# The first down product as seven products in turn, with its weight sums made in the projections

## What is computed

```python
h2 = _rmsnorm(x, norm2_w) * (1.0 + scale2) + shift2
ffn = jnp.dot(jax.nn.silu(jnp.dot(h2, w_ffn_gate)) * jnp.dot(h2, w_ffn_up), w_ffn_down)
x = x + gate2 * ffn
...
return _rmsnorm(x, final_norm_w)
```

## Time and profile before

| | |
|---|---|
| median of 3 runs | 1528.05 us (1527.63 to 1528.16) |
| profiled execution | 1528.31 us, span 1526.4 us |
| PE busy | 1509.9 us, 99% |
| DVE busy | 951.3 us, 62% |
| ACT busy | 634.2 us, 42% |
| transfers | 197.58 MB, mean 129 GB/s |

### The profile page before, as it was taken

The page is one execution under the profiler, slowest core; times in us unless marked ns, Lnnn a source line. Parts: engine busy times, 40 slices in busy tenths (PEclk is TensorE's granted clock), DMA queues, the critical chain, the costliest instruction groups (busy, mean ns, idle before and its releaser), DMA issues.

```text
span 1526.4 us, 21071 instructions
## 1 busy us (share of the span) xinstructions
PE 1509.9 (99%) x8593; PEld 1234.8 (81%) x8593; DVE 951.3 (62%) x1680; ACT 634.2 (42%) x1065; POOL 44.3 (3%) x82
## 2 busy tenths in 40 slices
PE   7999999999999999999999999999999999999999
PEld 5777887778888898888888887877788988888887
DVE  6679886765367666435333376787567456556885
ACT  4453334653322442222232253766525334434652
POOL 0000000000000000000000011200011000000000
PEclk9999999999999999999999999999999999999999
DMA  9322122136345258666522215100113232232463
GB/s 386 143 83 97 56 70 83 56 129 244 129 160 180 76 183 277 236 221 218 196 97 97 83 33 221 56 29 30 56 56 124 97 99 85 92 111 97 134 223 133
DMA packets 64042, 197.58 MB, mean 129 GB/s; under 512 B 5956, under 2 KB 6084, under 8 KB 62792
## 3 DMA queue, kind: packets, MB, share of 16 engines
q1 hardware_dynamic: 63944, 196.22, 37.3%
HBM read 182.57 MB, written 13.63 MB: 129 GB/s over the span
## 4 chain that ended last, share of the span: by engine, by line
PE 93%; DVE 4%; ACT 1%; DMA 1%; issue 1%; SPq 0%; DVEq 0%
PE bank L669 89%; PE bank L681 4%; DVE AR L1936 1%; DVE wl L1909 1%; DMA raw<-in_wst 1%; DVE G L1943 0%; DVE AR L2246 0%; DVE ST L1936 0%; DVE X L1936 0%; ACT AR L1779 0%; ACT wh L1370 0%; DVE Hl L1936 0%; ACT L1779 0%; DVE X L1943 0%; DVE PRMT L1936 0%
## 5 line engine op out<-in xcount | busy, mean ns | idle before, releaser
L1370 ACT ACTIVATE wh<-raw 128x1024 fp32r<-128x1024 f32 (+2 forms) x209 | 218.3, 1046 | 381.7 <-PE bank L669 331.9
L1909 DVE TENSOR_TENSOR wl<-raw,wh 128x1024 fp32r<-128x1024 f32 (+2 forms) x209 | 250.5, 1207 | 119.4 <-ACT wh L1370 119.2
L669 PE MATMUL bank<-wh,Hh 128*128 128x512 f32 (+1 forms) x758 | 305.4, 403 | 1.2 <-DVE Hl L1936 0.7
L669 PE MATMUL bank<-wh,Hl 128*128 128x512 f32 (+1 forms) x758 | 293.6, 387 | 0.0
L669 PE MATMUL bank<-wl,Hh 128*128 128x512 f32 (+1 forms) x758 | 292.8, 386 | 0.0
L669 PE MATMUL bank<-Hh,wh 128*128 128x512 f32 (+2 forms) x712 | 268.5, 377 | 0.2
L669 PE MATMUL bank<-Hl,wh 128*128 128x512 f32 (+2 forms) x712 | 266.9, 375 | 0.0
L669 PE MATMUL bank<-Hh,wl 128*128 128x512 f32 (+2 forms) x712 | 266.9, 375 | 0.0
L669 PEld LDWEIGHTS bank<-wh,Hh 128*128 128x128 f32 x758 | 142.5, 188 | 36.0 <-issue 9.8
L669 PEld LDWEIGHTS bank<-wh,Hl 128*128 128x128 f32 x758 | 142.3, 188 | 29.7
L669 PEld LDWEIGHTS bank<-wl,Hh 128*128 128x128 f32 x758 | 142.8, 188 | 24.7
(11 more groups left out here) (263 smaller groups left out, 1932.3 us busy)
## 6 DMA issues: line engine op xcount, KB each, us to landing
raw<-in_wst SPq DMA_DIRECT2D x246, 512.0 KB, 3.5
raw<-in_down SPq DMA_DIRECT2D x37, 512.0 KB, 5.7
sums_dram<-CST SPq DMA_DIRECT2D x11, 1024.0 KB, 7.9
raw<-sums_dram SPq DMA_DIRECT2D x20, 512.0 KB, 3.8
AR<-in_wst SPq DMA_DIRECT2D x8, 1024.0 KB, 11.6
X<-in_x SPq DMA_DIRECT2D x8, 512.0 KB, 5.8
AR<-in_wst SPq DMA_DIRECT2D x5, 512.0 KB, 5.2
out<-X SPq DMA_DIRECT2D x8, 256.0 KB, 2.1
```

The lines of the kernel that those rows point to most:

```text
L669: return e.matmul(o, l, r, start=start, stop=stop, skip_group_check=True)
L1370: e.activation(HI[slot[i]][:, 0:width(i)], raw[:, i % NR, 0:width(i)], ACT.Copy).then_inc(*w_hi.mark(i))
L1909: e.tensor_tensor(LO[slot[i]][:, 0:n], raw[:, i % NR, 0:n], HI[slot[i]][:, 0:n].bitcast(f32), SUB).then_inc(*w_lo.mark(i))
```

## The change

The first down product is done as seven products too. `SEVEN` becomes ("dn", "2dn"), so the weights of both come from their own tensors and there are 22 pairs. The pairs of dn are put behind chunks of gb1, ap, rp and wo (`PAIR_BEHIND`), those of 2dn are spread over up. The groups of left blocks are split from step 1 of dn on, the first four in up10, as they are for 2dn; for both products the groups 15 to 20 go to other buffers (`LEFT_IN`), two of them in the space of the activations. ACT copies the products "1", "7" and "6" out of their banks, DVE adds the others to the copies, multiplies by the gate and adds to x. Token tiles 0 and 1 are final at step 35, tile 2 at 42, tile 3 at 47, and `after_dn` gives their norms. The functions that the old product alone used are gone.

```diff
@@ -68,6 +68,14 @@
             plan.append((key, j, w, k, min(kt, first + rows - k), cols))
             if among and j >= start:
                 plan.append(among.pop(0))
+            if (key, j) in PAIR_BEHIND:
+                plan.extend(pair())
+
+    unsummed = [(key, p) for key in SEVEN for p in range(11)]
+
+    def pair():
+        key, p = unsummed.pop(0)
+        return [(key + side, p, None, 0, 2, [(0, 512)]) for side in "YX"]
 
     def ada(groups, kt):
...
@@ -89,16 +97,16 @@
         block(f"rp{n}", "w_ret_proj", 8, [(512 * n, 512)], among=among, start=1 - n)
     for n in (0, 1):
         block(f"wo{n}", "w_out", 8, [(512 * n, 512)], among=among)
-    among, first = ada((5,), 1), 11
+    among = ada((5,), 1)
+    turns = [1 + 43 * n // len(unsummed) for n in range(len(unsummed))]
     for j in range(11):
         for c in range(4):
             plan.append((f"up{j}", c, ("w_ffn_gate", "w_ffn_up"), 2 * c, 2, [(256 * j, 256), (256 * j, 256)]))
             if j > 1 and among:
                 plan.append(among.pop(0))
-            n, turn = divmod(4 * j + c - first, 3)
-            if turn == 0 and 0 <= n < 11 * len(SEVEN):
-                plan += [(SEVEN[n // 11] + side, n % 11, None, 0, 2, [(0, 512)]) for side in "YX"]
-    block("dn", "w_ffn_down", 22, [(0, 1024)], 1)
+            if 4 * j + c in turns:
+                plan += pair()
+    plan += seven_parts("dn")
     block("2kv", "w_in_2", 8, [(512, 512)])
     block("2kw", "w_in_2", 8, [(1024, 280), (2328, 16)])
     block("2nq", "w_in_2", 8, [(0, 512)])
@@ -119,7 +127,8 @@
 
 
 NR, NH, NP = 4, 4, 8
-SEVEN = ('2dn',)
+PAIR_BEHIND = {("gb1", 3), ("ap0", 1), ("ap1", 1), *((key, j) for key in ("rp0", "rp1", "wo0", "wo1") for j in (1, 3))}
+SEVEN = ("dn", "2dn")
 GROUPS = [("7", 0), ("7", 1), ("1", 0), ("1", 1), ("7", 2), ("1", 2)] + [(z, u) for z in "25634" for u in range(3)]
 
...
@@ -246,10 +255,6 @@
     def up(prefix):
         ticks.extend((prefix, (0, a, c), place[f"{prefix}0", c], a > 0) for a in (0, 256) for c in range(4))
         ticks.extend((prefix, (j, 0, c), place[f"{prefix}{j}", c], True) for j in range(1, 11) for c in range(4))
-
-    def down(key):
-        ticks.extend((key, (None, k), place[key, k], True) for k in range(16))
-        ticks.extend((key, (t, k), place[key, k], t == T - 1) for t in range(T) for k in range(16, 22))
 
     def seven(key):
...
@@ -315,7 +320,7 @@
                 while avail and avail[0][0] >= NH and not (place["up0", 0] <= at < place["2kv", 0] or at >= place["2up0", 0]):
                     avail.pop(0)
 
-                if name == "dn" and (what[1] < 21 and chunks[at][:2] == ("2kv", 2) or chunks[at][:2] == ("2kv", 3)):
+                if name == "dn" and chunks[at][0] == "2kv" and chunks[at][1] > 1 + (what[0] > 45):
                     break
                 ahead = 5 if name != "iq" else 3 if what[0] == 7 else what[0] % 2
...
@@ -584,7 +592,8 @@
         BANKS = {z: b for zs, b in (("74", (4, 5)), ("16", (6, 7)), ("2", (0, 1)), ("53", (2, 3))) for z in zs}
         PART = {"1": 0, "5": 0, "7": 1, "6": 1, "2": 2, "3": 2, "4": 3}
         BLOCK = {"dn": "up", "2dn": "2up"}
-        SPLIT_AT = {2 * n - 7: n for n in range(4, 21)}
+        SPLIT_AT = {**{2 * n - 7: n for n in range(4, 15)}, 25: 15, 27: 16, 29: 17, 31: 19, 32: 18, 33: 20}
+        LEFT_IN = [*range(5)] * 3 + [1, 2, 3, 5, 0, 6]
         SUMS_AT = {2: ("6", 0), 4: ("6", 1), 6: ("6", 2), 8: ("5", 0), 9: ("5", 1), 10: ("5", 2), 12: ("3", 0), 14: ("3", 1), 16: ("3", 2)}
 
...
@@ -600,7 +609,9 @@
         def split_left(n):
 
 
-            i = n % 5
+            i = LEFT_IN[n]
+            if i > 4:
+                return [LEFTS[:, o:o + 1024] for o in (2048 * i - 6144, 2048 * i - 5120)]
             return [EF[:, 0:1024] if i == 0 else h[:, 2 * i - 2:2 * i, :].rearrange("p a s -> p (a s)") for EF, h in ((EHF, Hh), (ELF, Hl))]
...
@@ -621,8 +632,13 @@
         def left_free(key, n):
 
 
-            z, u = GROUPS[n - 5]
-            return dense.of(("used", place[key + z, min(2 * u + 1, 5)] if n > 4 else place[BLOCK[key] + "10", n - 1]))
+            if LEFT_IN[n] > 4:
+                return dve.of((key, "left", 19))
+            earlier = [m for m in range(n) if LEFT_IN[m] == LEFT_IN[n]]
+            if earlier:
+                z, u = GROUPS[earlier[-1]]
+                return dense.of(("used", place[key + z, min(2 * u + 1, 5)]))
+            return dense.of(("used", place[BLOCK[key] + "10", n - 1]))
 
         DECAY = ((4, 5), (3, 6))
...
@@ -1052,7 +1068,7 @@
                         if last and c == 3:
                             free[b] = freed(j, m)
 
-            def seven(key, freed, each=lambda t: None):
+            def seven(key, freed, each=lambda s: None):
                 for s, z, g, rows in w.steps(key):
                     i = place[key + z, g]
...
@@ -1070,34 +1086,13 @@
                                 x.then_inc(*dense.mark(*events))
                             if p == 10 and (z, r) in freed:
                                 free[b] = freed[z, r]
-
...
 
             up("up", "n2", lambda j, m: (act.of(("up", "gate", 2 * j + m)) if m < 2 else dve.of(("up", "act", 2 * j + m - 2))), lambda: row_sum(5, (6, 7)))
-            down("dn", lambda t, n: dve.of(("dn", t, n)), lambda t: w.after(10, lambda: norm_turn("n3", t)))
+            taken = {("1", "p1"): act, ("7", "p7"): act, ("6", "u"): act, ("2", "c11 2"): dve, ("5", "v"): dve, ("3", "c12 3"): dve, ("4", "c21 4"): dve}
+            turns = {35: ((8, 0), (9, 1)), 42: ((10, 2),), 47: ((10, 3),)}
+            seven("dn", {(z, r): on_engine.of(("dn", event, r)) for (z, event), on_engine in taken.items() for r in (0, 1)},
+                  lambda s: [w.after(n, lambda t=t: norm_turn("n3", t)) for n, t in turns.get(s, ())])
 
             H3 = lambda t: dve.of(("n3", "low", t))
...
@@ -1677,40 +1667,34 @@
                             on.wait_ge(*dve.of(("up", "act", k - 4)))
                         e.activation(SGR[k % 4], bank[up_bank(j, m)][:, :], ACT.Silu).then_inc(*act.mark(("up", "gate", k)))
 
-            def down(key, of, last_group, evac):
-                def split(k):
-                    if k < 2 or k > 21:
-                        return
-                    s = k % 8
-                    on.wait_ge(*dve.of((of, "act", k)))
-                    on.wait_ge(*last_group)
...
-                w.after(10, lambda: norm_gain("n3", t, dense.of(("dn", t, 1))))
-
-            down("dn", "up", dense.of(("up", 10, 3)), after_dn)
+                w.after((3, 4, 4, 4)[t], lambda: norm_root("n3", t, dve.of(("last", "x", t))))
+                w.after((7, 8, 10, 10)[t], lambda: norm_gain("n3", t, dense.of(("dn", "3", 1))))
+
+            def take(z, event, to, ready):
+                for r in (0, 1):
+                    on.wait_ge(*dense.of(("dn", z, r)))
+                    on.wait_ge(*ready(r))
+                    e.activation(to[r], bank[BANKS[z][r]][:, :], ACT.Copy).then_inc(*act.mark(("dn", event, r)))
+
+            for s, z, g, rows in w.steps("dn"):
+                if s in SPLIT_AT:
+                    left_high("dn", SPLIT_AT[s])
+                if s == 14:
+                    take("1", "p1", SGR[0:2], lambda r: dve.of(("up", "act", 21)))
+                if s == 16:
+                    take("7", "p7", SGR[2:4], lambda r: dve.of(("up", "act", 21)))
+                if s == 32:
+                    take("6", "u", SGR[0:2], lambda r: dve.of(("dn", "c11", r)))
+                for t in {36: (0, 1), 42: (2,), 47: (3,)}.get(s, ()):
+                    after_dn(t)
 
             def keys_square(name, e_key):
...
@@ -2415,57 +2399,71 @@
...
                     w.settle()
                 if (j, a, c) == (6, 0, 0):
                     take_rows(5, (6, 7), dve.now())
                 if (j, c) == (10, 0):
-                    early_low("up")
+                    left_low("dn", 0)
+                if j == 10 and c > 0:
+                    left_low("dn", c)
                 if c == 3 and (j or a):
                     for m in (0, 1):
                         k = 2 * j + m
                         on.wait_ge(*act.of(("up", "gate", k)))
...
+                        if m == 0:
+                            left_difference("dn", j)
 
             def after_dn(t):
-                for n in (0, 1):
-                    residual(SGR[(2 * t + n + 2) % 4], ("dn", t, n), n, t, 2 * t + n, ("dn", t, n), ("dn", "x", t) if n else ("dn", "x0", t))
-
                 def last_norm():
                     ss = ST[:, 20 + t:21 + t]
                     on.wait_ge(*pool.of(("last", "root", t)))
                     on.wait_ge(s_bc, 32)
                     stt(X[:, t, :], X[:, t, :], ss, BC[:, :], MUL, MUL, ("last", "x", t))
-                w.after(4, last_norm)
-                w.after(7, lambda: norm_scale("n3", t))
-                w.after(10, lambda: norm_gain("n3", t))
-                w.after(11, lambda: norm_low("n3", t))
-
-            down("dn", after_dn)
```

(45 more changed lines are left out.)

73 lines of the change are left out of this document (9 added, 64 removed).

## The result

The changed kernel takes 1567.76 us (median of 4 runs, 1566.22 to 1569.41), the kernel before 1528.09 beside it: a ratio of 1.026, 95% interval 1.0243 to 1.0278. It is 2.6% slower, 39.7 us more. 1538.5 was predicted, in a range of 1521 to 1551: the sign holds, and the time lies 17 us outside the range.

The account below looks back on a forecast made before the run. TensorE, busy 99% of the span, was taken as the bound. Losses of 3.6 + 6.4 + 5.1 + 4.3 + 5 + 1 = 25.4 us against 15.0 won gave 10.4 more: 1538.5 us, range 1521 to 1551.

Parts of the forecast that it names:

- Removed, 15.0: Down product: 462 matmuls instead of 528, 66 fewer at 0.2267 us each, 15.0 us less TensorE time.
- A: In ap0: a pair waits for the store before it, delaying y's tile 0 low part; TensorE loses 3.6 us.
- B: In wo0: a pair waits for the store before it, delaying merged tile 6's low part; TensorE loses 6.4 us.
- C: In wo1: a pair waits for the store before it, delaying tile 0's residual and norm; TensorE loses 5.1 us.
- rival (1): Stores land sooner in the projections; at 4.5 us the time is 1523.5 us. Chance 0.12.
- D: In up0: two pairs and a weight low part put ahead of n2's last low part; TensorE loses 4.3 us.
- E: Between ap0 and wo0: close pairs delay bank merges and loads; nothing if DVE catches up, else 9 us; taken at 5.
- The tail: End of the first down product: tile 0's chain of 8.6 us against 8.8; 0 to 3 us lost, taken at 1.
- Rival (3): Granted clock falls after waits of this length: ten slow matmuls after each of five, 10 us, 1549 us. Chance 0.08.
- refill: Not in the prediction: estimate after measuring, about 0.16 us more for each of 15 TensorE waits, 2.4 us.
- Rival (2): TensorE does not meet the waits because the pairs are spread otherwise: the 15.0 stand, 1513 us. Chance 0.10.
- Rival (4): Transfers become the bound in rp0 to wo0, 382 GB/s: 12 us more than the sum, 1551 us. Chance 0.06.

Follow-up runs that it names:

- sums alone: The kernel before, old down product kept, with the first product's eleven pairs summed and stored at the change's places but not used: 1574.27 us.
- product alone: The changed kernel without the first down product's sums: plain weights of the same size are read instead; 1522.0 us, ratio 0.9945 to 0.9975.
- three reorderings: DVE's tail reordered: six operations to steps 36 and 37 (1522.9 us) or further back (1524.55), both without sums; norm low parts later, whole change (1531.44).
- spread in threes: The changed kernel with nine pairs ahead of up, thirteen in it mostly three chunks apart, and six tail operations moved further back: 1532.27 us.
- spread: The changed kernel with nine pairs from the gates' stages to wo0 and thirteen in up, three chunks apart: 1538.32 us.
- tail's second order: Six DVE operations of the down product's tail moved behind the last two closings: 1524.55 us with plain weights for sums, 1532.27 in the whole change.
- product alone, tail 2: The changed kernel with plain weights for sums and six tail operations moved behind the last two closings: 1524.55 us, ratio 0.9966 to 0.9985.

## Why the prediction was right in sign and wrong in size

**Removed, 15.0: right.** 421 matmuls in 95.36 us are 0.2265 each.

**A, B, C: right in size, and in mechanism for A and mostly for C.** Predicted 3.6, 6.4 and 5.1, measured 3.36, 7.05 and 5.04, each behind a pair that waits for the store before it. The store's landing, 7.9, refutes rival (1). But the prediction has all of each from the store. Where nothing is stored, A is gone and C falls from 5.05 (in the sums alone) to 1.49, but B only from 7.96 to 4.20, and to 1.31 with the arithmetic gone too. So about half of B has another source, DVE's work and late loads, and that its size came out is in part luck.

**D: right in mechanism, under-sized.** 4.3 predicted, 7.6 of waits measured, and the run with the two pairs put back shows that it is theirs. I had DVE's work, 5.5 and 1.2, but not that the second pair would wait 3.08 us for its loads (580.25).

**E: taken at 5, measured 9.6,** just over the far end of 9. The reason I gave was DVE catching up or not. What the runs show beside it is the load side: ACT waits up to 11.32 us for a weight, and up to 8.07 in the kernel that only loads the pairs. Of the same waits, 8.8 in the sums alone, 5.1 are left without stores and 3.8 with loads only. The prediction named SP's queue there and gave it no price of its own.

**The tail: taken at 1, bound 3, measured 7.35.** This is the step of the product, "covered by 105 us of matmuls", that was wrong. My chain of 8.6 us against 8.8 counted what tile 0 needs and nothing that DVE has to do besides. DVE's timeline of the change:

```profile
907.99 0.68 DVE L1920 TENSOR_TENSOR AR<-AR 128x512 f32<-128x512 f32 x1
...
917.98 0.69 DVE L1920 TENSOR_TENSOR X<-X,AR 128x512 f32<-128x512 f32 x1
918.59 1.82 DVE L1893 TENSOR_TENSOR wl<-raw,wh 128x1024 fp32r<-128x1024 f32 x2
```

From the first row to the second, twelve closing operations of 0.7 us and two weights' low parts stand one behind the other without a gap; the low parts that TensorE wants come behind them, and it waits until 919.86. The product alone has 7.3 us of these waits with no pair near. The three reorderings show that it isn't the place of the six operations alone; which part of the chain would have to be shorter stays open.

**The granted clock: the failed step with the largest price.** Rival (3) had the mechanism, 10 us and a chance of 0.08; the forecast itself had it at nothing. Measured 12.4. The ground for nothing was a misreading: that the clock is 1.00 "even after the 9 us before the first matmul". TensorE's timeline of the kernel before, at that place:

```profile
8.99 4.53 PE L681 MATMUL bank<-CST,AR 128*128 128x128 f32 x24 [8.99 <-DVE AR L1939]
...
14.45 1.09 PE L681 MATMUL bank<-CST,AR 128*128 128x128 f32 x8
```

These are the same transposes. 24 take 4.53 us where 8 take 1.09 later: their starts are 0.213 us apart until 12.4, then 0.109. That is half clock behind an idle time of 9 us. The windows' column shows 1.00 there because the trace's record of the clock begins only at 12.5 us. So the kernel before had the answer in the distance of starts, where the column had none. The rule of the Trainium skill cited there (TensorE: Matmul & The Clock Gate, Part 1, an idle TensorE is throttled) agrees with the changed kernel's trace: granted clock 0.74 and 0.88 in the windows around a wait of 7.05 us. The kernel before agrees too, by the starts above, so it was wrong to say that its trace neither shows nor excludes the rule. I had listed the rule and the waits side by side and treated them as alternatives, though the rival's condition was my own forecast.

By terms, measured less predicted: A to D 23.05 - 19.4 = 3.65; E 9.6 - 5 = 4.6; tail 7.35 - 1 = 6.35; clock 12.4; refill 2.4. That is 29.4 over a forecast of 10.4: 39.8, where the spans have 39.9. The prediction had no term for the refill. Rival (2) is refuted by the idle times. Rival (4) is refuted as put: its 382 GB/s throughout are not reached, no window shown moves more than 309, and the fullest 10 us (460 to 470) move 350. But the rate is not cleared of a part, since there the DMA engines are busy 96% and loads land later (5.8 us against 4.2). How much of the lateness is the order of issue with four raw buffers and how much the rate was not separated.

The range was too narrow because its high end took only part of rival (3). E and the tail at their far ends (1544.5) with rival (3) on top is 1554.5, still 13.3 short: 4.35 from the tail, whose bound of 3 had no row behind it, 3.65 from A to D, 2.4 each from clock and refill, and 0.6 from E.

## What to carry to other kernels

Work that fits an engine by its busy share still costs when it stands in order ahead of something due: price for each inserted step the buffers it holds and the loads that queue behind them, not only its arithmetic and its store. In this kernel every run with waits of 4 us or more on TensorE also had stretches at half clock, so a forecast that has the first must carry the second in its sum. Read the clock at a place by the distance of starts too, not by the column alone. Where a chain ends a stage, count everything its engine has to do in that stretch, not the chain alone.

## What was not expected of the hardware

The granted clock fell to half around waits as short as 1.94 us (569.42 in the change) and 1.77 (473.84 in the whole kernel spread in threes), and in the change 12.4 us went there, nearly a third of the loss. A wait's length alone doesn't decide. Wait A, 3.36 us in the change, left the clock at 1.00, and the same wait with 3.42 us in the sums alone did not. The clock stayed at 1.00 through the tail of the profiled product alone, with five waits of 0.88 to 2.58 us in 23 us, and fell for 3.4 us in that of the kernel "spread" behind the same first wait of 2.58. With the tail's second order it stayed through a wait of 3.38 in the product alone and fell around one of 3.41 in the whole kernel. Executions of one and the same kernel differ as well: 1.000 once and 0.997 or 0.998 nine times for the product alone, tail 2. What decides between these was not found.

The fall also makes waits cost more than their rows: two pairs with 9.0 us of waits in up0 cost 10.8.
